# One routed-experts stage, its tensor-engine order regrouped and its row gathers bounded

## What is computed

```python
def swiglu(x, wg, wu, wd):
    return (jax.nn.silu(x @ wg) * (x @ wu)) @ wd
...
def routed_experts(h, eidx, gate_w, w_e_gate, w_e_up, w_e_down, blk):
    ...
    def expert_block(args):
        tok, e = args
        return swiglu(h_pad[tok], w_e_gate[e], w_e_up[e], w_e_down[e])

    ys = lax.map(expert_block, (row_tok.reshape(n_blocks, blk), block_e)).reshape(n_rows, D)
    out = jnp.zeros((M + 1, D), ys.dtype).at[row_tok].add(ys * row_w[:, None])
```

## Time and profile before

| | |
|---|---|
| median of 3 runs | 2266.12 us (2264.55 to 2268.11) |
| the profiled execution, its own time | 2270.59 us |
| its span, first to last instruction | 2268.8 us |
| busy share of the span | PE 93%, DVE 61%, ACT 46%, POOL 46% |
| mean granted TensorE clock | 0.969 of full speed |
| routed experts (first turn L2507 to the last put) | from 1356.5 us on, about 890 us |
| blocks run (scatters L2472 in the trace) | 66 |
| share of the chain that ended last | L2545 16%, L2573 8%, L2532 6%, L2518 3%, L2583 3%, L2507 1%, L2559 1%, L2557 1% |

### The profile page before, as it was taken

How to read it: one execution, slowest core, us unless ns; L and a number is a source line. 1 busy time by engine, 2 the same in 40 slices (tenths; PEclk the granted TensorE clock), 3 DMA queues, 4 the chain that set the end, 5 groups by cost and what they waited for, 6 DMA issues and landing times. The chain is left out here.

```text
span 2268.8 us, 42925 instructions
## 1 busy us (share of the span) xinstructions
PE 2109.6 (93%) x15302; PEld 1587.1 (70%) x15302; DVE 1380.3 (61%) x2383; ACT 1047.1 (46%) x1584; POOL 1036.6 (46%) x850
## 2 busy tenths in 40 slices
PE   7999889979799989999898989999999999999994
PEld 6777667756444448888677647777777777777773
DVE  3487778875576662111257537777777767777772
ACT  6321212256566661111233116666666666666662
POOL 2111212343578741101006514677676766766662
PEclk9999999979799999999999999999999999999997
DMA  6587811055555556883333258999999999999996
GB/s 221 168 262 237 262 61 38 17 166 164 192 164 168 166 188 222 290 276 105 131 144 100 95 191 298 340 335 331 338 340 331 333 337 341 328 338 336 339 327 157
DMA packets 178690, 520.62 MB, mean 229 GB/s; under 512 B 22907, under 2 KB 77354, under 8 KB 152142
## 3 DMA queue, kind: packets, MB, share of 16 engines
q1 hardware_dynamic: 130070, 355.43, 44.6%
q0 software_dynamic: 37520, 97.81, 16.9%
q10 hardware_dynamic: 10992, 66.02, 8.6%
HBM read 442.31 MB, written 125.08 MB: 250 GB/s over the span
## 5 line engine op out<-in xcount | busy, mean ns | idle before, releaser
L2696 DVE TENSOR_TENSOR w_gu_lo<-turned,w_gu_hi 128x2048 fp32r<-128x2048 f32 x132 | 302.5, 2293 | 148.4 <-ACT w_gu_hi L2618 148.4
L2618 ACT ACTIVATE w_gu_hi<-turned 128x2048 fp32r<-128x2048 f32 x132 | 253.9, 1924 | 40.3 <-PEq L1898 40.3
L612 PE MATMUL pP<-wring,hT_hi 128*128 128x512 f32 (+2 forms) x576 | 229.1, 398 | 22.2 <-DVE wring L547 11.9
L613 PE MATMUL pP<-wring,hT_hi 128*128 128x512 f32 (+2 forms) x576 | 223.4, 388 | 0.0
L614 PE MATMUL pP<-wring,hT_lo 128*128 128x512 f32 (+2 forms) x576 | 223.0, 387 | 0.0
L2545 PE MATMUL pG_e<-w_gu_hi,xT_hi 128*128 128x512 f32 x528 | 214.6, 406 | 0.0
L2545 PE MATMUL pG_e<-w_gu_lo,xT_hi 128*128 128x512 f32 x528 | 208.7, 395 | 0.0
L2545 PE MATMUL pG_e<-w_gu_hi,xT_lo 128*128 128x512 f32 x528 | 208.6, 395 | 0.0
L2472 POOL DMA_INDIRECT x_scratch<-turned,target x66 | 106.9, 1620 | 194.9 <-ACT turned L2659 194.9
L476 ACT ACTIVATE stage<-pP 128x512 f32<-128x512 f32 (+3 forms) x72 | 41.1, 571 | 310.5 <-PE pP L614 299.4
L2458 POOL DMA_INDIRECT turned<-h_scratch,index x64 | 170.2, 2659 | 20.0 <-issue 20.0
(11 more groups left out here) (335 smaller groups left out, 5070.7 us busy)
## 6 DMA issues: line engine op xcount, KB each, us to landing
turned<-in_w_e_up SPq DMA_DIRECT2D x65, 1024.0 KB
turned<-in_w_e_down SPq DMA_DIRECT2D x65, 1024.0 KB
turned<-in_cache_sb_kv SPq DMA_DIRECT2D x256, 256.0 KB, 3.1
turned<-in_w_e_gate SPq DMA_DIRECT2D x64, 1024.0 KB
out<-in_cache_win_kv ACTq DMA_DIRECT2D x8, 4094.0 KB
turned<-in_w_in ACTq DMA_DIRECT2D x56, 256.0 KB, 6.6
turned<-in_w_in SPq DMA_DIRECT2D x16, 512.0 KB, 7.9
out<-in_cache_win_kv ACTq DMA_DIRECT2D x8, 1022.0 KB
```

Source lines behind the costliest of these rows:

```text
L612: pe.matmul(pP[:m, i % 4, :w], hi, w_hi(u), start=(c == 0), stop=False)
L613: pe.matmul(pP[:m, i % 4, :w], hi, w_lo(u), start=False, stop=False)
L2618: act.activation(ghi[:, r, k, :, :].rearrange("p c f -> p (c f)"), w[:, r, k, :], ACT.Copy).then_inc(ghi_ready, 1)
L2696: dve.tensor_tensor(glo[:, r, k, :, :].rearrange("p c f -> p (c f)"), w[:, r, k, :], ghi[:, r, k, :, :].rearrange("p c f -> p (c f)").bitc ...
```

## The change

On PE the order within a block's turn is written anew: `turn_hidden` of the block before, `turn_tail` and `turn_rows` of the next block together, then `down_tail` and `gate_up_tail` together, then `gate_up` and `down`. `down_tail` of a block moves from behind `turn_hidden` to behind the turns. ACT and DVE take the high and low parts of the turned rows ahead of the tail's silu and product. The two gathers of POOL get a bound: an index beyond the last real row moves nothing.

```diff
-                    pool.indirect_dma_start(rows[r], None, sc["h2"], bass.IndirectOffsetOnAxis(ap=index[:, r, 0:1], axis=0)).then_inc(rows_in[r], 16)
-                    pool.indirect_dma_start(tail[r], None, h2_quarters, bass.IndirectOffsetOnAxis(ap=index[:, r, 1:2], axis=0)).then_inc(rows_in[r], 16)
+                    pool.indirect_dma_start(rows[r], None, sc["h2"], bass.IndirectOffsetOnAxis(ap=index[:, r, 0:1], axis=0),
+                                            bounds_check=T - 1, oob_is_err=False).then_inc(rows_in[r], 16)
+                    pool.indirect_dma_start(tail[r], None, h2_quarters, bass.IndirectOffsetOnAxis(ap=index[:, r, 1:2], axis=0),
+                                            bounds_check=QT * T - 1, oob_is_err=False).then_inc(rows_in[r], 16)
...
                     for j in range(U):
-                        turn_next = which != "last" or j < U - 1
-                        if turn_next:
+                        if which != "first" or j > 0:
+                            turn_hidden(it, j - 1)
+                        if which != "last" or j < U - 1:
                             turn_tail(it, j + 1)
+                            turn_rows(it, j + 1)
+                        if which != "first" or j > 1:
+                            down_tail(it, j - 2)
                         gate_up_tail(it, j)
-                        if turn_next:
-                            turn_rows(it, j + 1)
                         gate_up(it, j)
                         if which != "first" or j > 0:
                             down(it, j - 1)
-                        turn_hidden(it, j)
-                        if which != "first" or j > 0:
-                            down_tail(it, j - 1)
...
                 body(last, "last")
+                turn_hidden(last, U - 1)
+                down_tail(last, U - 2)
                 down(last, U - 1)
                 down_tail(last, U - 1)
...
                     for j in range(U):
-                        gate_tail(it, j)
                         if which != "last" or j < U - 1:
                             rows_high(it, j + 1, 0)
                             rows_high(it, j + 1, 1)
+                        gate_tail(it, j)
+                        if which != "last" or j < U - 1:
                             gu_high(it, j + 1, 0)
                         gate(it, j)
...
                     for j in range(U):
+                        if which != "last" or j < U - 1:
+                            rows_low(it, j + 1, 0)
+                            rows_low(it, j + 1, 1)
                         gate_tail(it, j)
                         if which != "last" or j < U - 1:
                             take_tail(it, j + 1)
-                            rows_low(it, j + 1, 0)
-                            rows_low(it, j + 1, 1)
                             gu_low(it, j + 1, 0)
                         gate(it, j)
```

## The result

The changed kernel is slower. Over 20 runs of each its median is 2268.64 us against 2263.53 for the kernel before: ratio 1.0022, 95% interval 1.0013 to 1.0030, 5.0 us. One slow run of the changed kernel, of 2997.24 us, counts in its median but not in the ratio. I had forecast 6.3 us less. The single profiled execution of the changed kernel is shorter than that of before (span 2265.7 against 2268.8 us), and the first thing to see is that this comes from ahead of the changed stage.

The account below looks back on a forecast made before the run. PE, busy 400.00 of 400.00 us in the routed experts, was taken as the bound. Terms of -8.2 and +1.9 us summed to -6.3; shifted from the profiled execution to the runs' median, 2259.8 us, range 2256 to 2269.

Parts of the forecast that it names:

- PE's saving: PE's small pieces in each routed-expert turn: one width change fewer, -0.13 us a turn (0.09 to 0.17), 63 turns, 8.2 us less.
- The beginning: Block 0's `gate_up_tail` moves behind block 1's `turn_rows`, out of PE's idle time: +1.9 us, bounds 1.6 to 2.6.
- what is moved past others: Later `y_ready` and weight loads, earlier gather requests, reordered ACT and DVE work: covered by slack, 0 us; uncovered, at most 70.
- the DMA engines hold the turn: Routed-expert turns: the two queues' 102% share keeps them at 13.27 us, only the slower beginning remains, 2268.0 us; chance 0.24.
- POOL's bounded gathers: POOL's two gathers: bounded form costs 2.9 us more each, POOL's round passes PE's turn, about 2398 us; chance 0.08.
- The clock did not fall: PE's grouped small work: a rival had the clock falling in each group, +77 us, about 2337 us; chance 0.04.
- The slower outcome: Whole kernel measurably slower, beyond about 0.2% (4.5 us): POOL, the clock and 0.01 for the unseen; chance 0.13.
- the signs of being wrong: New profile: turn still 13.27 us with PE gaps behind DMA, PE gaps ending with `put`, or turns shorter than 13.1.
- The bounds at 0: POOL's bounded gathers: 22% of gathered bytes go, saving DMA engines 4% of their time; PE waits for none, worth 0.

Follow-up runs that it names:

- after_y2: The changed kernel with a second `y` (and `y_tail`) buffer, used in turn, so `put` waits for the scatter two blocks back; ratio 0.9985 to the kernel before.
- half_weights: The changed kernel, single `y`, each weight load after the first loop round fetching only half its columns (outputs not the reference's); ratio 0.9985 to the kernel before.
- bounds_only: The kernel before, order untouched, with only the bounds on POOL's two gathers added; ratio 0.9999 to the kernel before.
- before_y2: The kernel before with a second `y` (and `y_tail`) buffer, used in turn; ratio 0.9987 to the kernel before.
- three_widths_y2: The changed kernel with two `y` buffers, the old beginning, and PE's small work as turns, `turn_hidden`, `down_tail`, `gate_up_tail`; ratio 0.9924 to the kernel before.

## Why the prediction was wrong

**PE's saving: right, a little too large.** `down_tail` to `gate_up_tail` is 0.89 us (forecast 0.88), `gate_up_tail` to `gate_up` 1.96 (1.94), the ten turns 1.24 (1.24), the first `gate_up` distance 0.34 (0.34). The sum is -0.11 a turn, not -0.13, inside the bounds, 7.3 us in all by the 13.16 us turn. Where the scatter is taken out of the way, after_y2 and half_weights show it: 6.2 us less in 63 turns than the kernel before.

**The beginning: right mechanism, 2.5 us for 1.9**, near the upper bound of 2.6, since the whole piece ran with the clock still low: `gate_up_tail` to `gate_up` took 1361.44 - 1358.71 = 2.73 us. The granted clock from 1355 to 1362 us was 0.61:

```profile
1355.00:1362.00 7.00, 5.18 (x74) 4.41 (x75) 3.31 (x7) 1.62 (x4) 3.47 (x4) 0.61 0.32 86
```

**The step that failed** is the one on what is moved past others: "y_ready comes 1.1 us later in the turn", the slack of 10.9 us for the down weights, and "I cost all these at nothing; without this cover each would cost its own delay". The delay was forecast nearly right (1.1 us; the down load is issued 1.3 us later), and the weights did come in time. But the cover was counted for the loads' own reader only. I did not ask who else needed the DMA engines in those microseconds, although the two queues' shares summed to 102%. The scatter's packets stood behind the later loads, and their landing, not `y_ready`, released `put`. `put` was already waiting before, 162 us in the rows above; I read `put` as waiting for `y_ready` and `target` and left its third wait, `y_out`, out. I had put this term at nothing; it was 9.0 us of stretched turns, against 7.3 won. The sum lacked two sizes behind `y_out`: 4.26 us from `put` to the scatter's issue and 8.7 us until it has landed, together 13.0 of a 13.27 us turn before the change.

**The rivals.** That the DMA engines hold the turn was nearest to the truth, but I had thought of it as throughput, which could only cancel the gain. It works by latency through one single buffer, so it can cost more than the gain. POOL's bounded gathers cost the program nothing (bounds_only); the shortest L2457 is 1.03 us with the bound, 0.98 without. But POOL's own work, which I summed to 9.4 us from an early block, is longer in the steady turns, where it meets DVE. L2458 takes 2.66 us there on average, not 0.96. Before:

```profile
1810.05 2.29 DVE L2696 TENSOR_TENSOR w_gu_lo<-turned,w_gu_hi 128x2048 fp32r<-128x2048 f32 x1 [1.31 <-ACT w_gu_hi L2618]
1810.35 2.85 POOL L2458 DMA_INDIRECT turned<-h_scratch,index  x1 [0.31 <-issue]
```

In each of 57 turns this gather ends 0.85 to 0.87 us after DVE's 2.29 us instruction, as if it began only then, and in all but one the copy of `target` ends 0.05 us after the next of that length. `target`, for which `put` waits, is made late by that; no run tried what it would bring to take it away. The clock did not fall: 1.00 in the window above, with twelve turns and two small products in one row. The fall for which the Trainium skill spoke (TensorE: Matmul & The Clock Gate, Part 4) does not show here. The slower outcome had 0.13, 0.12 of it on those two; the true mechanism was only among the signs of being wrong ("PE shows gaps that end with POOL's or ACT's `put`").

**The bounds at 0** held in the old order, where no landing is late enough to hold PE, and not in the new one, where they bring about 0.2%. They free less of the DMA engines than the 4% that I had: the queues' shares together fell from 102.0 to 100.9% over 50 turns of bounds_only, while the software queue's packets stayed as many (23,856 for 23,857).

**What stays open.** Whether the scatter's packets yield to the loads inside the DMA engines, or in the memory behind them, no run separates; half_weights changes both. How the loss divides between the down load and those of gate and up is not shown either. Nor was a version tried that issues the scatter ahead of the gate and up loads.

## What to carry to other kernels

When an edit makes a semaphore later, follow it into every DMA that is issued behind it, and ask of each not only when its own reader wants it, but which other transfer shares the engines then and who waits for that one's landing. A wait that is already in the list with 2 to 3 us a time, on an engine with plenty of idle time, is a loop with little slack; a second buffer there is cheap insurance before PE's order is tightened (1.0022 became 0.9985, and 0.9981 became 0.9924). And where an engine is bound by pieces of different width, count the changes in the whole cycle: with two buffers, five to four brought 0.07 us a turn (before_y2 to after_y2) and four to three 0.16 (to three_widths_y2).

## What the hardware showed that I had not expected

The software queue moves little while the hardware queue has loads pending: 5 packets against 159 in 3 us with two scatters just issued, 17 against 122 in half_weights from 2.3 us after the issue on. The Trainium skill, DMA: Bandwidth & Descriptors, Queues, rings and completion order, says that each engine takes turns between its queues packet by packet. By that rule the software queue would have had a good part of the packets while both had work; the counts do not show it, though how much of the scatter was ready to move in these windows is not shown.

Loads issued 1.0 us (gate) and 2.3 us (down, 0.59 us ahead of `gate_up` where it was 2.93) later, by one wait on SyncE, cost 29 us of a 2264 us program, by way of a 1.1 us copy on an engine that is idle for a third of the time.
